# A hybrid decoder trunk's attention bias, read from a table repeated 128 times in device memory in place of flip matmuls and copies

## The reference

```python
dist = qi + C_BLOCK - kj
valid = (dist >= 0) & (dist <= span) & (blk * C_BLOCK + kj - C_BLOCK >= 0)
bias = table[t5_bucket(jnp.maximum(dist, 0) * dil)].transpose(2, 0, 1).astype(f32)
s = jnp.einsum('brhnqd,brhnkd->brhnqk', qb, kb).astype(f32) * (D ** -0.5) + bias[:, None]
s = jnp.where(valid, s, -jnp.inf)
```

## Time and profile before

| | us |
|---|---|
| runs, median of 3 (lowest to highest) | 2117.56 (2116.93 to 2118.57) |
| the profiled execution, its own time | 2120.26 |
| its span, from first to last instruction | 2118.5 |
| TensorE busy (share of the span) | 2027.8 (96%) |
| VectorE busy | 1609.6 (76%) |
| ScalarE busy | 1233.7 (58%) |
| GpSimd busy | 16.5 (1%) |

### The profile page before, as it was taken

One profiled execution on the slowest core, in us unless ns is written; L12 is line 12 of the kernel. 1 busy time (PEld: TensorE's weight loads), 2 busy tenths in 40 slices (PEclk: granted clock), 3 DMA queues, 4 the chain that ended last, 5 costly groups with the idle time before them and its releaser, 6 DMA issues.

```text
span 2118.5 us, 28922 instructions
## 1 busy us (share of the span) xinstructions
PE 2027.8 (96%) x10759; PEld 1728.0 (82%) x10759; DVE 1609.6 (76%) x1256; ACT 1233.7 (58%) x1013; POOL 16.5 (1%) x22
## 2 busy tenths in 40 slices
PE   7999999989997999999979999999999999999997
PEld 6998888879997988888868878888887888888885
DVE  5878865755445878955766888898888889888985
ACT  4544455444433554455446777777777777777774
POOL 0000000000000000000000000000000000000000
PEclk9999999999999999999988999999999999999999
DMA  8523455245554522455247999999999999999994
GB/s 279 160 80 100 140 178 179 89 151 188 179 190 136 177 82 90 145 164 186 91 149 260 387 344 378 359 362 368 353 379 341 382 358 364 375 341 372 351 375 179
DMA packets 240481, 516.97 MB, mean 244 GB/s; under 512 B 11519, under 2 KB 34167, under 8 KB 240412
## 3 DMA queue, kind: packets, MB, share of 16 engines
q1 hardware_dynamic: 238124, 507.60, 68.1%
q0 software_dynamic: 2288, 8.41, 1.1%
HBM read 513.86 MB, written 2.12 MB: 244 GB/s over the span
## 4 chain that ended last, share of the span: by engine, by line
PE 87%; DVE 7%; ACT 3%; issue 2%; DMA 0%; SPq 0%; DVEq 0%; ACTq 0%
PE PS L476 25%; PE PS L478 25%; PE PS L477 25%; PE PS L547 7%; DVE lo L1533 2%; ACT hi L1102 2%; PE PS L1002 1%; PE PS L978 1%; PE PS L496 1%; PE PS L758 0%; DVE a_act L1634 0%; DMA rows<-in_knorm_c 0%; PE PS L948 0%; PE PS L789 0%; DVE t_n L1556 0%
## 5 line engine op out<-in xcount | busy, mean ns | idle before, releaser
L1533 DVE TENSOR_TENSOR lo<-raw,hi 128x2048 fp32r<-128x2048 f32 x481 | 1095.0, 2290 | 295.0 <-ACT hi L1102 292.3
L1102 ACT ACTIVATE hi<-raw 128x2048 fp32r<-128x2048 f32 x481 | 919.6, 1915 | 337.8 <-PE PS L478 330.5
L476 PE MATMUL PS<-hi,e_hi 128*128 128x512 f32 x896 | 355.3, 397 | 1.4 <-DVE e_lo L1556 1.4
L478 PE MATMUL PS<-hi,e_lo 128*128 128x512 f32 x896 | 350.2, 391 | 0.0
L477 PE MATMUL PS<-lo,e_hi 128*128 128x512 f32 x896 | 350.2, 391 | 0.0
L476 PE MATMUL PS<-hi,actT_hi 128*128 128x512 f32 x640 | 253.9, 397 | 4.6 <-DVE lo L1533 4.1
L478 PE MATMUL PS<-hi,actT_lo 128*128 128x512 f32 x640 | 249.6, 390 | 0.0
L477 PE MATMUL PS<-lo,actT_hi 128*128 128x512 f32 x640 | 249.1, 389 | 0.0
L476 PE MATMUL PS<-hi,fT_hi 128*128 128x512 f32 x536 | 210.6, 393 | 9.8 <-DVE fT_lo L1556 9.3
L477 PE MATMUL PS<-lo,fT_hi 128*128 128x512 f32 x536 | 209.5, 391 | 0.0
L478 PE MATMUL PS<-hi,fT_lo 128*128 128x512 f32 x536 | 209.3, 390 | 0.0
(11 more groups left out here) (323 smaller groups left out, 2153.8 us busy)
## 6 DMA issues: line engine op xcount, KB each, us to landing
raw<-in_moe_w SPq DMA_DIRECT2D x336, 1024.0 KB, 5.8
raw<-in_w_in SPq DMA_DIRECT2D x92, 1024.0 KB, 5.2
raw<-in_ffn_w SPq DMA_DIRECT2D x33, 1024.0 KB, 5.3
raw<-in_w_br SPq DMA_DIRECT2D x12, 1024.0 KB, 5.0
raw<-in_w_out SPq DMA_DIRECT2D x8, 1024.0 KB, 5.2
hankel<-hankel_dram POOLq DMA_DIRECT2D x1, 1536.0 KB, 13.6
x<-in_x SPq DMA_DIRECT2D x2, 512.0 KB, 4.0
gain<-in_norm_mix POOLq DMA_DIRECT2D x2, 512.0 KB, 5.8
```

What stands on the lines that cost most here:

```text
L476: pe.matmul(out, a_hi, b_hi, start=first, stop=False, skip_group_check=True)
L478: return pe.matmul(out, a_lo, b_hi, start=False, stop=last, skip_group_check=True)
L1102: act.activation(hi[prog.u % SPLIT][:, :], raw[slot][:, :], COPY).then_inc(hi_made.sem, 1)
L1533: dve.tensor_tensor(lo[prog.u % RAW][:, :], raw[prog.u % RAW][:, :], hi[s][:, :].bitcast(F32), ALU.subtract).then_inc(lo_made.sem, 1)
```

## The change

The flip tile, `spread_bias`, `bias_copies`, `hankel` and their semaphores go. The GpSimd queue writes `by_dist` to device memory 128 times over, one copy per partition, in three DMAs, one per group. With a copy per partition, a row can be read with a step of one copy less one element, which takes the start of a row back by one element per partition: the rows land in `bias` in the wanted order by one DMA. ScalarE gets a wait for the three stores ahead of the tanh into `b_q` in layer 0, and VectorE a wait for the load ahead of `scaled(0)` in layer 0.

```diff
-K_ID, K_LE, K_GT, K_M0, K_MT, K_FLIP, K_N = 0, 1, 2, 3, 4, 11, 12
+K_ID, K_LE, K_GT, K_M0, K_MT, K_N = 0, 1, 2, 3, 4, 11
...
-    tiles.append(i + j == P - 1)
...
-    hankel = sb("hankel", [P, GROUPS * H, T], at=u1 + 12288 + 8192)
...
-    hankel_dram = nc.dram_tensor("hankel_dram", (GROUPS * H, DIST), F32, kind="Internal").ap()
+    by_dist_dram = nc.dram_tensor("by_dist_dram", (GROUPS * H, P, DIST), F32, kind="Internal").ap()
...
-        def spread_bias(first):
-
-            pe.wait_ge(ab_read.sem, ab_read.at(0))
-            pe.wait_ge(hankel_here.sem, 16)
-            for n in range(first, first + 3):
-                if n >= 3:
-                    pe.wait_ge(bias_kept.sem, n - 2)
-                mm(PS[:, 4 + n % 3, :], consts[:, K_FLIP, :],
-                   hankel[:, 2 * n:2 * n + 2, :].rearrange("p a b -> p (a b)")).then_inc(bias_done.sem, 1)
...
-                if g and L == 0:
-                    spread_bias(3 * (g - 1))
...
-            pe.wait_ge(*((ab_read.sem, ab_read.at(L)) if L else (bias_kept.sem, 4)))
+            pe.wait_ge(ab_read.sem, ab_read.at(L))
...
-                        if L == 0:
-                            pe.wait_ge(bias_kept.sem, 6)
...
-            def bias_copies(L, first):
-                if L == 0:
-                    for n in range(first, first + 3):
-                        act.wait_ge(bias_done.sem, n + 1)
-                        act.activation(bias[:, 2 * n:2 * n + 2, :].rearrange("p a b -> p (a b)"),
-                                       PS[:, 4 + n % 3, :], COPY).then_inc(bias_kept.sem, 1)
...
-            bias_copies(L, 0)
...
-            bias_copies(L, 3)
...
             used(L, 10)
+            if L == 0:
+                act.wait_ge(by_dist_out.sem, 16 * GROUPS)
             act.activation(b_q[:, :, :].rearrange("p a b -> p (a b)"),
...
+            if L == 0:
+                dve.wait_ge(bias_here.sem, 16)
             scaled(0)
...
         pool.wait_ge(by_dist_kept.sem, 1)
-        pool.dma_start(hankel_dram.rearrange("(g h) z -> h g z", g=GROUPS), by_dist[:, :, :])\
-            .then_inc(by_dist_out.sem, 16)
-        pool.wait_ge(by_dist_out.sem, 16)
-
-        pool.dma_start(hankel[:, :, :], bass.AP(hankel_dram.tensor, 0, [[1, P], [DIST, GROUPS * H], [1, T]]))\
-            .then_inc(hankel_here.sem, 16)
+        for g in range(GROUPS):
+            pool.dma_start(by_dist_dram[g * H:(g + 1) * H, :, :],
+                           by_dist[:, g, :].unsqueeze(1).broadcast_to([H, P, DIST])).then_inc(by_dist_out.sem, 16)
+        pool.wait_ge(by_dist_out.sem, 16 * GROUPS)
+
+        pool.dma_start(bias[:, :, :], bass.AP(by_dist_dram.tensor, P - 1,
+                                              [[DIST - 1, P], [P * DIST, GROUPS * H], [1, T]]))\
+            .then_inc(bias_here.sem, 16)
```

More of the change, by code:

```diff
@@ L297, in build @@
     by_dist_out = signal("by_dist_out")
-    hankel_here = signal("hankel_here")
-    bias_done = signal("bias_done")
-    bias_kept = signal("bias_kept")
+    bias_here = signal("bias_here")
     ab_split = signal("ab_split")
```

## The result

The changed kernel takes 2190.91 us, the median of four runs (2188.03 to 2192.8), against 2118.07 us before (four runs, 2116.93 to 2118.62): a ratio of 1.0342, 95% interval 1.0328 to 1.0357, or 72.8 us more. The profiled execution took 2189.71 us and has a span of 2187.9. The two profiled executions differ by 69.4 us of span, since the one before ran longer than its median and the one after shorter. The sign of the forecast was right and its size was not: 2131.6 us, with a range that ended at 2160.

A forecast was written before the change was run, and what follows sets the result against it. TensorE was taken as the bound, VectorE close behind. Stores ending at 109.1 us would delay unit 12 by 14.0 us, swallowing the 3.4 us gain: span 2118.5 + 14.0 = 2132.5, median 2131.6 us, range 2112.8 to 2160.

The forecast's parts named there:

- What bounds the kernel: Whole kernel: TensorE is 87% of the chain; in the first 120 us VectorE is a second path with almost no slack.
- Removed from TensorE, and what VectorE leaves of it: Flip matmuls near 48 and 62 us: 5.16 us removed, of which VectorE's low parts leave a lead of 3.31 us.
- How long does the store take: Three stores from partitions 0 to 3: 2.36 MB at one engine's pace, 27.1 GB/s, ending at 109.1 us.
- The likeliest case: Early layer 0: store bound by its source, loads little touched; 2131.6 us, own range 2122 to 2140, chance 0.38.
- the sign that the prediction gave for the starved case: ScalarE's weight splits: ScalarE waiting for raw weights ahead of 90 us would show that the stores starve the weight loads.
- the ScalarE wait: Before layer 0's tanh into b_q: held until the stores end, unit 12 following 6.7 us later, +14.0 us.
- The rival of the starved loads: Weight loads during the stores: slow packets hold their engines, unit 8 multiplied at 113 us; +37 us, 2155; chance 0.26.
- The hidden store: Before layer 0's b_q tanh: stores at 37 GB/s or more end by 86.2 us; 2114.2 us, or 2112.3; chance 0.36.

## Why the prediction was wrong

*What bounds the kernel.* Right: TensorE with VectorE close behind. *Removed from TensorE, and what VectorE leaves of it.* Near: a lead of 3.3 us forecast, after three small waits; 2.8 to 3.1 in four runs. Removing work from the engine that makes up 87% of the chain gave 60% of it.

*How long does the store take.* Right in its rate: 25.6 GB/s against 27.1; ended at 119 us against 109.1. Of the missing 10 us, 5.8 are the data (92.2 us against 86.4) and the rest lies behind it: the first packet ran at 22.2 us, as forecast (22.7), the last ended at 114.4, and its landing came 4.8 us later. The forecast had such a time once, ahead of the data. The rate rested on a guess, that four neighbouring partitions "should be served by one such share" of sixteen, and the Trainium skill, "SBUF — State Buffer", Door 1: The DMA port swizzle, gave 27.6 GB/s for these partitions; the runs with one, two and four of its ports gave 25.6, 51.6 and 92.

*The likeliest case.* This is the step that failed: "with loads little touched". It priced the store by its effect on ScalarE, the one engine that waits for it, and took the other users of the DMA engines to be nearly free of it. The stores held 11.5 engines, the weights were held with them (ScalarE waited 81.5 us for units 3 and 4, ahead of 110 us: the sign that the prediction gave for the starved case), and the ScalarE wait, on which the sum rests, cost nothing. With one store at a time it is worth what I worked out (6.54 against 6.7 us from its end to unit 12).

*The rival of the starved loads* was the mechanism, at 0.26 and mis-sized: +37 us against +72.8. Two terms. The ratio of 1.78 to 1 came from a window of 25 to 31 us in which the hankel load had moved nothing by 27.4 us, so it counts time in which the weights ran alone. With both queues full, in 29 to 33 us, the same trace has

```profile
q0 software_dynamic: 231, 0.95, 65.2%
q1 hardware_dynamic: 232, 0.48, 36.2%
```

one weight row of 2 KB for each packet of 4 KB, 0.5 to 1, as one row to one packet of 4.6 KB, 0.44 to 1, beside the slow store. By that, the stores' 43 packets an engine let 43 rows of an engine's share through, 1.3 units, where the forecast has 5.3 units. And I asked when unit 8 would be there, the last that fits into the store's time by my ratio; with the right one it is unit 4, which is complete only when the stores leave the engines, at 109 us, and is wanted about 36. 109.17 - 36.30 (ScalarE's start of it before) = 72.87, the whole loss of VectorE. The rival's sum, 2155 us, lay inside the stated range but outside the likeliest case's own, and the chance on it was too low: each row I had for contention (two queues sharing, each at its engines' pace) said that a queue takes its share of an engine's time, and a packet from a slow source takes more of it.

*The hidden store* (0.36) would have needed 37 GB/s. With 92 GB/s, four paths, it is still not hidden, because in 25 us of held engines ScalarE waited 8.7 us for a unit. With all partitions as the source it is: 2117.16 us (one run) with all 2.36 MB, 2116.39 with 32 copies, against the 2114.2 of the case. What those runs have more, a copy on VectorE ahead of the table and 12 loads in place of one, the case did not have. The lower end of the stated range, 2112.8, is neither of the case's own two sums (2114.2 and 2112.3), and nothing in the prediction gives it.

The low clock in the idle stretch (0.50 granted between 50 and 75 us, the level of 1.2 GHz, with TensorE at rest) costs little: it was back at 1.00 in 130 to 140 us, while VectorE was still the limit, and the flips' 3.07 us at 169.01 are what the other runs have.

## To carry over

A transfer's price is not only its own time. Ask which partitions it reads or writes, how many engines it occupies for how long, and what else those engines bring; the one that suffers is the one with the least slack, not the one that waits for it. A share of the engines far above a queue's share of the bytes (72% for 26 GB/s) is the sign. And a ratio between two queues is to be read from a window in which both are full from end to end, and in packets: here it was one to one, whatever their sizes and however slow one of them was.

To repeat a small table in device memory, compute it on all partitions first (the matmuls with 128 columns took 4.21 us, those with four 4.00), and let the store run from all of them.

## What the runs showed of the hardware

- Partitions 0 to 3 together give 25.6 GB/s to DMA reads; 0, 33, 66, 99 give 51.6; 0, 5, 10, 15 give 92.
- An engine is held by a packet from a slow source for as long as it takes: 2.06 us in the mean for 4.6 KB with 12 engines on one path, 0.67 us with four. Meanwhile the other queue passes one packet a turn: 54 rows of 2 KB beside 55 store packets, and 232 beside 231 packets of 4 KB in the kernel before. The Trainium skill, "DMA: Bandwidth & Descriptors", Queues, rings and completion order, says that each engine takes turns between its queues by whole packets; both counts agree with that.
- Three DMAs with four rows outermost held 11.5 engines together and 3.6 one at a time. The Trainium skill, "DMA: Bandwidth & Descriptors", Rules for kernel authors, says that an outermost dimension below 16 confines a DMA to at most as many engines; both figures agree.
- A wait of 7.43 us for the weights fell into loads of 16 partitions each; in loads of 32 no wait fell, but the weights were slow there as well (18.9 us a unit).
